# A feed-forward block in two stages through device memory, with seven-product multiplication on 512-token halves

## The reference

```python
h = _rmsnorm(x, P['norm_ffn_g'][layer]) * (1 + mod[:, 4]) + mod[:, 3]
gu = h @ P['ffn_w_gate_up'][layer]
x = x + mod[:, 5] * ((jax.nn.silu(gu[..., :FFN_HIDDEN]) * gu[..., FFN_HIDDEN:]) @ P['ffn_w_down'][layer])
```

## Time and profile before

| what | value |
|---|---|
| median of 3 runs | 2457.27 us (2455.51 to 2458.7) |
| the profiled execution's own time | 2461.06 us |
| its span, first to last instruction | 2459.3 us |
| PE busy | 2393.5 us (97%) |
| PEld (weight loads) busy | 2277.0 us (93%) |
| DVE, ACT, POOL busy | 1171.8, 693.8, 767.3 us |
| mean granted TensorE clock | 0.988 |

### The profile page before, as it was taken

The page is one execution under the profiler, slowest core; times in us unless marked ns, Lnnn a source line. Parts: engine busy times, 40 slices in busy tenths (PEclk is TensorE's granted clock), DMA queues, the critical chain, the costliest instruction groups (busy, mean ns, idle before and its releaser), DMA issues.

```text
span 2459.3 us, 37048 instructions
## 1 busy us (share of the span) xinstructions
PE 2393.5 (97%) x15703; PEld 2277.0 (93%) x15703; DVE 1171.8 (48%) x2225; ACT 693.8 (28%) x1056; POOL 767.3 (31%) x650
## 2 busy tenths in 40 slices
PE   7999998999999999999999999999999999999998
PEld 5997877678999999999999999988999999999998
DVE  5277653456444444344445411546544444444445
ACT  5122233426322222122224311144412222122224
POOL 3221120113244333334333332122443333433431
PEclk8999999999999999999999999999999999999999
DMA  9424342861221222222222678311111111111111
GB/s 305 161 67 144 118 138 77 295 236 35 69 86 57 79 71 86 69 86 86 69 86 69 213 269 296 119 36 35 35 52 46 41 52 52 35 52 52 52 52 71
DMA packets 163969, 249.12 MB, mean 101 GB/s; under 512 B 6164, under 2 KB 150825, under 8 KB 162526
## 3 DMA queue, kind: packets, MB, share of 16 engines
q1 hardware_dynamic: 150762, 179.29, 22.2%
q0 software_dynamic: 4784, 63.31, 7.4%
q10 hardware_dynamic: 8260, 4.15, 0.6%
HBM read 228.04 MB, written 62.54 MB: 118 GB/s over the span
## 4 chain that ended last, share of the span: by engine, by line
PE 76%; DVE 2%; ACT 1%; issue 0%; ACTq 0%; DVEq 0%
PE ps L2832 32%; PE ps L2872 12%; PE ps L2870 11%; PE ps L2871 11%; PE ps L3023 3%; PE ps L2976 3%; PE ps L3158 1%; DVE x L1870 1%; PE ps L3046 0%; PE ps L3350 0%; PE ps L3193 0%; PE ps L3367 0%; DVE nt L1909 0%; DVE tmp L2430 0%; PE ps L3313 0%
## 5 line engine op out<-in xcount | busy, mean ns | idle before, releaser
L2832 PE MATMUL ps<-h_hi,w_slot 128*128 128x352 f32 x2112 | 539.3, 329 | 6.1 <-ACT tmp L1389 2.9
L2630 POOL TENSOR_TENSOR w_slot<-w_raw,w_slot 128x512 fp32r<-128x512 f32 x240 | 303.9, 1298 | 682.0 <-DVE w_sum L2023 555.5
L2832 PE MATMUL ps<-f_hi,w_slot 128*128 128x352 f32 x1920 | 470.3, 324 | 0.0
L2872 PE MATMUL ps<-h_hi,w_slot 128*128 128x352 f32 x1280 | 413.3, 323 | 0.0
L2870 PE MATMUL ps<-h_hi,w_slot 128*128 128x352 f32 x1280 | 412.9, 323 | 0.0
L2871 PE MATMUL ps<-h_lo,w_slot 128*128 128x352 f32 x1280 | 411.2, 321 | 0.0
L1960 DVE SCALAR_TENSOR_TENSOR x<-ps,mod,x 128x704 f32<-128x704 f32 (+1 forms) x384 | 270.5, 746 | 290.8 <-PE ps L2832 290.2
L2832 PEld LDWEIGHTS ps<-h_hi,w_slot 128*128 128x128 f32 x2112 | 371.8, 189 | 25.3 <-issue 21.9
L2616 POOL TENSOR_TENSOR w_slot<-w_raw,w_slot 128x512 fp32r<-128x512 f32 x132 | 177.6, 1372 | 535.7 <-ACT w_slot L1384 527.2
L2832 PE MATMUL ps<-h_lo,w_slot 128*128 128x352 f32 x1056 | 340.2, 322 | 0.0
L2832 PEld LDWEIGHTS ps<-f_hi,w_slot 128*128 128x128 f32 x1920 | 334.2, 188 | 4.9 <-issue 4.1
(11 more groups left out here) (398 smaller groups left out, 3215.0 us busy)
## 6 DMA issues: line engine op xcount, KB each, us to landing
w_raw<-in_ada_w SPq DMA_DIRECT2D x48, 1024.0 KB, 6.0
w_raw<-in_ffn_w_gate_up SPq DMA_DIRECT2D x44, 1024.0 KB, 5.1
out_kv_sample<-in_cache_b_kv POOLq DMA_DIRECT2D x8, 4088.0 KB, 20.7
w_raw<-in_ffn_w_down SPq DMA_DIRECT2D x22, 1024.0 KB, 4.9
w_raw<-in_e_w_in SPq DMA_DIRECT2D x11, 1024.0 KB, 5.5
w_raw<-in_o_w_in SPq DMA_DIRECT2D x10, 1024.0 KB, 16.2
cache<-in_cache_b_kv SPq DMA_DIRECT2D x16, 512.0 KB, 6.1
out_kv_sample<-in_cache_b_kv POOLq DMA_DIRECT2D x8, 1016.0 KB, 8.8
```

The costliest lines, as they stand in the source:

```text
L2630: pool.tensor_tensor(w_slot[slot_of(it.raw)][:, c], w_raw[it.raw.slot][:, c], w_slot[it.hi[0]].bitcast(F32)[:, c], ALU.subtract).then_inc( ...
L2832: mm = pe.matmul(big(t)[:, b, 0:BLK], wt, xt[:, k, b * BLK:b * BLK + BLK], start=(k == 0 and n == 0), stop=(k == K - 1 and n == 2))
L2872: return pe.matmul(bank(it, j), w_low, x_high, start=False, stop=last, skip_group_check=True)
```

## The change

The feed-forward block goes in two stages.

Stage one makes gate and up of groups 1 to 10 as 20 units, one after the other, without down units between them. Each has seven products on the two halves of 512 prompt tokens, 84 matmuls of 512 columns; there is no direct block. The order of the products is 1, 2, 6, 4, 7, 5, 3, and products 6 and 7 accumulate in the PSUM bank of product 1, which ScalarE copies out after each of the three (`sum_copied`). Each unit uses three banks; the next uses the other three. Hidden values are stored to a scratch tensor in device memory, group by group, by SP (`store_f`), from the tile in which the next gate unit will write.

Stage two has 10 down units per layer for the hidden groups 0 to 9: five chunks of 512 hidden rows, each with two halves of 512 output channels. A chunk (2 MB) is loaded back by SP into the space of h_lo (`load_chunk`). VectorE makes four token sums of it (two operations of `chunk_sums` in each of two items), ScalarE five high parts (`chunk_high`), and GpSimd and VectorE the low parts. A down unit is 14 products of 6 matmuls of 512 columns, 84 in all, two output pairs (q) side by side in six banks. VectorE adds each product straight into x (`added`): 8 additions of 512 columns and 4 of 1,024 per unit. The down rows of group 10 stay a plain unit.

Samples leave the dense matmuls. For each seven-product unit they are the 32-column weights of full-float matmuls over 256 columns of the raw weight tile, packed in four column groups as the modulation units are: 8 matmuls and 2 transposes for a gate or up unit, twice 4 matmuls and 2 transposes for a down unit. ScalarE copies the rows, and VectorE reduces four partial sums. They read the raw weights, so they stand after product 6 of the unit before.

The modulation units of layer 0 stand after products 4 and 7 of units 1 to 10, two to a unit, and their weights go into the space of x, which is stored to memory at the start of the block and loaded back in unit 14.

The diff, cut to its core (`it` is a unit, `after` the next one, `before` the one before, `lefts` the count of VectorE's writes up to a unit):

```diff
+GATE_ORDER = (1, 2, 6, 4, 7, 5, 3)
+DOWN_ORDER = (1, 2, 6, 4, 5, 7, 3)
...
+        units = [seven(role, layer, g) for g in range(1, GROUPS) for role in ("f_gate", "f_up")]
+        units += [down_seven(layer, c, h) for c in range(CHUNKS) for h in range(2)]
...
+            for which in DOWN_ORDER if down else GATE_ORDER:
+                if which == 3 and after:
+                    sums_split(after)
+                items.append(Item("product", of=it, which=which))
...
+                elif which == 6 and after:
+                    sample_of(after)
+                elif which == 4:
...
+                    if after:
+                        split(after)
...
+                release(slot_of(it.raw), product_last(it, 4))
+                release(it.hi[0], product_last(it, 4))
...
+                release(it.sums[0], product_last(it, 3))
+                release(it.sums_hi[0], product_last(it, 3))
...
+            def store_f(layer, g, m):
+
+                sp.dma_start(d_f[:, 2 * g + m, :], tmp[:, m, :]).then_inc(f_stored, 16)
+
+            def load_chunk(it):
...
+                sp.dma_start(xr[:, 0:4, c], rows[:, :, FIRST]).then_inc(chunk_loaded[it.j % 2], 16)
+                sp.dma_start(xr[:, 4:8, c], rows[:, :, SECOND]).then_inc(chunk_loaded[it.j % 2], 16)
...
+                if which == 2:
+                    if it.role == "f_gate":
+                        dve.wait_ge(f_stored, 32 * (10 * it.layer + it.j))
+                    else:
+                        dve.wait_ge(gate_made, 10 * it.layer + it.j)
+                    dve.wait_ge(copied, 3 * it.n + 1)
+                    summed(it, 1, part_a, tmp_c11)
...
+                def added(q, m, c, src):
+
+                    m += 4 * it.g + 2 * q
+                    dst = x[:, m, c]
...
+                    dve.scalar_tensor_tensor(dst, src, mod[:, 6 * layer + it.gate, m, 0:1], dst, ALU.mult, ALU.add)\
+                        .then_inc(banks_left, 1)
...
+                    if which == 1:
+                        if first:
+                            pe.wait_ge(*all_left(before))
+                        else:
+                            pe.wait_ge(banks_left, before.lefts + 9 + q)
+                        pe.wait_ge(*left_low(2))
+                        pe.wait_ge(part_made, 4 * it.r + 2)
+                        straight(it, 0, q, 0, 0, rows(0))
...
+                    elif which == 6:
+                        pe.wait_ge(t_made, made + 5)
+                        pe.wait_ge(banks_left, it.lefts + 1 + q)
+                        of_sums(it, 0, q, 1, sums(T2), adds=True)
...
+                for k in range(count):
+                    j = S_TOK * (k % 4)
+                    mm = pe.matmul(misc(it.misc)[j:j + S_TOK, 0:256], rows[:, k, :], w[:, k, c],
+                                   start=(k < 4), stop=(k >= count - 4), skip_group_check=True)
+                mm.then_inc(misc_ready, 1)
```

More of the change, by code:

```diff
@@ L201, in make_plan @@
 def make_plan():
-    n = {"unit": 0, "big": 0, "misc": 0, "norm": 0, "seven": 0, "part": 0}
+    n = {"unit": 0, "big": 0, "misc": 0, "norm": 0, "seven": 0, "part": 0, "gu": 0, "fd": 0, "done": 0, "left": 0}
     def take(what, count=1):
@@ L521, in seven, with down_seven @@
         col = g if role == "f_gate" else GROUPS + g
-        return Item("seven", weights="ffn_w_gate_up", col=col, role=role, layer=layer, j=g, n=take("seven"))
+        return Item("seven", weights="ffn_w_gate_up", col=col, role=role, layer=layer, j=g, n=take("gu"), w=take("seven"),
+                    done=take("done", 7), lefts=take("left", 6))
+    def down_seven(layer, c, h):
+        return Item("seven", weights="ffn_w_down", role="f_down", layer=layer, j=c, g=h, gate=5, n=take("fd"), w=take("seven"),
+                    done=take("done", 14), lefts=take("left", 12))
     def split(it):
@@ L527, in split @@
         items.append(Item("split", of=it))
-        for half in range(2 if it.kind == "seven" else 0):
+        for half in range(2):
             items.append(Item("w_sums", of=it, which=half))
@@ new lines, in ffn, with adds, chunk @@
+        sums_split(units[0])
+        def adds(i, which):
+            if layer or not 1 <= i <= 10:
+                return
+            if which in (4, 7):
+                ada_units.append(Item("ada", k=len(ada_units), misc=take("misc")))
+                items.append(ada_units[-1])
+            else:
+                items.append(Item("ada_out", k=len(ada_units) - 1, misc=take("misc")))
+        def chunk(kind, c, which=0):
+            if c < CHUNKS:
+                items.append(Item(kind, layer=layer, j=c, which=which))
@@ L986, in build_trunk @@
         for i, it in enumerate(plan):
-            if it.kind == "down_tile":
+            if it.kind == "product":
                 break
@@ L1701, in _ @@
                     split_hi(ups[it.layer].unit + 1)
[L1702 to L1706 removed]
+                elif it.kind == "product" and it.of.role != "f_down":
+                    gate_product(it.of, it.which)
                 elif it.kind == "project":
@@ new lines, in product, with summed @@
+            def product(it, which, q=0):
+                dve.wait_ge(*product_done(it, which, q))
+            def summed(it, j, part, dst):
+                if it.role == "f_gate":
+                    dve.tensor_tensor(dst, bank(it, j), part, ALU.add).then_inc(banks_left, 1)
+                    return
+                to = bank(it, j) if dst is tmp_c21 else part
+                own(dve.tensor_tensor(to, bank(it, j), part, ALU.add))
+                dve.tensor_tensor(dst, to, dst, ALU.mult).then_inc(banks_left, 1)
@@ new lines, in three, with straight @@
+            def three(it, j, q, w_high, w_low, x_high, x_low, first, last):
+                pe.matmul(bank(it, j, q), w_high, x_high, start=first, stop=False, skip_group_check=True)
+                pe.matmul(bank(it, j, q), w_high, x_low, start=False, stop=False, skip_group_check=True)
+                return pe.matmul(bank(it, j, q), w_low, x_high, start=False, stop=last, skip_group_check=True)
+            def straight(it, j, q, k0, m, x, adds=False):
+                down = it.role == "f_down"
+                hi, lo = [w_slot[s].rearrange("p (k n) -> p k n", k=4 if down else KT) for s in (it.hi[0], slot_of(it.raw))]
+                count, m = 2 if down else 4, m + 2 * q
+                for k in range(count):
+                    x_high, x_low = x(k)
+                    c = slice(m * P, m * P + P)
+                    mm = three(it, j, q, hi[:, k0 + k, c], lo[:, k0 + k, c], x_high, x_low, k == 0 and not adds, k == count - 1)
+                mm.then_inc(products_done, 1)
@@ new lines, in of_sums @@
+            def of_sums(it, j, q, i, x, adds=False):
+                down = it.role == "f_down"
+                hi, lo = [w_slot[s].rearrange("p (s k n) -> p s k n", s=4, k=4) for s in (it.sums_hi[0], it.sums[0])]
+                pe.wait_ge(part_made, 4 * it.rs + (DOWN_SUMS if down else GATE_SUMS).index(i) + 1)
+                count = 2 if down else 4
+                for k in range(count):
+                    x_high, x_low = x(k)
+                    n = 2 * k + q if down else k
+                    mm = three(it, j, q, hi[:, i, n, :], lo[:, i, n, :], x_high, x_low, k == 0 and not adds, k == count - 1)
+                mm.then_inc(products_done, 1)
```

809 lines of the change are left out of this document (494 added, 315 removed).

## The result

The changed kernel takes **2542.0 us** (median of 4 runs, 2540.6 to 2549.0) against 2456.4 before (4 runs beside it): ratio 1.0358, 95% interval 1.0345 to 1.0371, so 3.6% slower. I had forecast 2414, faster, with 2458 as the upper end. The profiled execution has a span of 2540.2 us. SBUF is the on-chip memory in which the tiles stand, and PSUM holds TensorE's results, in banks.

A forecast was written before the change was run, and what follows sets the result against it. TensorE, busy 97% of the span, was taken as the bound. Per layer, dense gain 84.0 less samples 44.0 gave 80 in all; less stalls of 37, net 43: 2461.1 to about 2418, median 2414 us, range 2362 to 2458.

The forecast's parts named there:

- What a matmul costs: Dense matmuls of 512 columns: 0.227 us each, with a fixed surplus per matmul; dense gain 84.0 us per layer.
- Rival B: Weight load sets the pace now, so a 512-column matmul costs 0.2133 to 0.216; 2361 us, chance 0.18.
- Samples: Separate sample matmuls: 1.34 us per gate or up unit, 1.72 per down unit; cost 44.0 us per layer.
- Rival E: Four column groups of samples run one after another, 60 units x 2 us more; 2534 us, chance 0.01.
- (c): Down units: TensorE waits ahead of product 6 for VectorE's addition of product 1, 0.8 us at 8 places; 6.4 us.
- (d): Stall at the last additions before the final down unit: 0.9 x 2 = 1.8 us.
- (f): Gate units: the first sum waits until the hidden tile is stored, delaying product 4; 0.4 x 20 = 8 us.
- rival C: Gate units' wait for the stored hidden tile costs 3.2 us more each, 64 in all; 2478 us, chance 0.10.
- (a): Start of each block: product 6 waits behind ScalarE's high parts and copy of product 1; 3.3 x 2 = 6.6 us.
- (b): Passage from gate and up to down units: VectorE's queue of 14.1 us outlasts TensorE's 9.5; 4.6 x 2 = 9.2 us.
- (e): Layer 0's gate units 1 to 10: modulation weights land late in SP's queue; 5 us in all.
- Rival D: VectorE paces stage two: operations cost 10% more, each down unit waits 1.5 to 2 us; 2449 us, chance 0.11.

The follow-up runs named there:

- e1: Changed kernel with the seven products of layer 1's gate and up units cut to seven widths, 256 to 512 columns: 2473.5 us.
- e11: Changed kernel with stores on ScalarE's queue, first sums' high part earlier, token sums moved and GpSimd's row pieces split: 2484.0 us, ratio 1.0100.
- e7: Changed kernel with the first chunk's token sums made 4 us earlier, directly after the weight sums of the first down unit: 2553.0 us.
- e3: Changed kernel with 16 of GpSimd's 24 pieces per pair of down units cut to 16 columns: 2497.7 us, pair 45.5 us.
- e5: Changed kernel with ScalarE making the first weight sums' high part earlier at each block's start, ahead of T3's: 2533.0 us.
- e14: e13 with token sum T3 of the next chunk moved to the pair's second unit and GpSimd starting with rows 2 and 3: 2482.1 us.
- e9: Changed kernel with 16 of GpSimd's 24 subtractions per pair of down units replaced by full-size one-operand copies: 2512.0 us.
- e13: e11 with the chunk loads after the first issued from ScalarE's queue instead of SP's: 2488.6 us, ratio 1.0143.
- e4: Changed kernel with the stores of hidden rows issued by ScalarE instead of SP: 2529.8 us.

## Why the prediction was wrong

The miss is 2542 - 2414 = 128 us. By its steps, with what the trace shows for both layers together:

- **What a matmul costs.** The step that failed first. I took the fixed surplus, 0.227; it is 0.232, close to the proportional end, and e1 shows the proportion for seven widths. 5,040 x 0.005 = **25 us**. The reason I gave, that short full-float records come every 0.117 us, told of weight loads and nothing of whether the surplus goes by columns. Rival B, which lies on the other side, is refuted with it. So is, for this stream, the N / 2.4 + 2.5 ns of the Trainium skill's "TensorE: Matmul & The Clock Gate", section "Back-to-back issue gap".
- **Samples.** A gate or up unit 20.83 - 84 x 0.2325 (the distance within a product of that unit) = 1.30 against 1.34: right. A clean down unit (the last full one of e11, 21.45) 1.92 against 1.72: 4 us over 20 units. Rival E is out.
- **(c) Down units.** Predicted 6.4; measured 251.5 (from 2240.8 to 2492.3) - 10 x 21.45 = 37.0 per layer, 74 in all: **68 us**, half of the miss. The wait of (d) stands behind that stretch, 1.2 a layer against 0.9: **1 us**. I had the queue and its order right, even the place (product 6 waits for product 1's addition) and the number of times (8), but summed VectorE's instructions by durations taken in a gap where nothing ran beside them: 4.6 us for token sums that take 7.0, an end 0.8 us late that came 4.1 late. The step that failed is the unwritten one, that VectorE at 87% and GpSimd at 74% (24 pieces of 1.29 in two units) do not touch each other. By the sizes in this trace VectorE's instructions of a pair with two operands in SBUF are 7 x 1.22, 8 x 0.69 and 4 x 0.22, 14.9 us, and GpSimd's 24 pieces 30.2: together 45.1 of a clean pair's 42.9. This sum is an estimate, and somewhat high, since the two overlap a little where they meet: in e7 a sum and a piece by turns take 2.2 us and not 1.22 + 1.26. It says that there is hardly a place where a piece stands free; it is no floor that a run has shown. With GpSimd's pieces whole no pair in the middle of a block took less than 47.2; e3, at 45.5, had made two thirds of them nearly nothing. And a stall of 4 us brings half a clock with it, 2 us more, which I had in no term.
- **(f) Stores.** 8 predicted, 18 measured (0.6 to 0.9 in most gate units, up to 2.3, by their length beside an up unit's), **10 us**. That is rival C's mechanism, and its sign came in 18 of 20 gate units; but it would have needed 44 us more than my 8 to take the forecast gain.
- **(a) Starts** 6.6 predicted, 5.9 + 6.5 measured, the 4.7 us gap and the half clock behind it: **6 us**. e5 shows the chain was the one I named.
- **(b) Passage** 9.2 predicted, a gap of 8.8 instead of 0.2 per layer, 17.2, measured: **8 us**; T1 took 2.22 and a sample addition 0.98 there, beside GpSimd.
- **(e) Modulation weights** 5 predicted, no hole found. But the step "the modulation units move without a change in number, 0" was wrong: an up unit of layer 0 with its two takes 23.72, 2.89 more than one without, and in the earlier trace rows two of them cost 67.81 - 65.60 = 2.21. Standing singly costs 0.7 in each of 10 units, **7 us**, less the 5: 2.

These sum to 25 + 4 + 68 + 1 + 10 + 6 + 8 + 2 = 124 of 128. The other 4 I have not placed.

Rival D had the right engine, "VectorE paces stage two", and its sign came, a hole before product 6 in all 20 down units (4.1 us in eight of them). It had 2449 for it: it took 10% on each instruction where the trace shows 85% on those beside GpSimd. The range ended past D and left out C; nothing in it held several terms going wrong in one direction, and they did. For (c), the largest, the reason is shown: its durations came from rows of a stretch in which nothing or little ran beside them.

The gain side was also thinner than it looked. With 0.232 dense work per layer is 585, not 572, and with samples (26 + 19) 630 against 656: 26 us per layer, 52 in all, in exchange for every stall. The stalls that e11 did not remove (4.7 x 8 for pairs, 17 for passages) are 55 us by themselves. So the best versions found, e11 and e14, are still 1.0 and 1.2% slower than the kernel before by their runs; none of the 14 is faster, not even those that leave work out.

## What to carry to other kernels

Before adding work to VectorE or GpSimd, add up, per stage, VectorE's instructions with two operands in SBUF and GpSimd's that read SBUF (e9's copies with one operand count too), and hold the sum against the stage's length as if they were one engine; if it comes near, there is hardly a place where the two do not meet; a duration from a stretch where the other is silent is a lower bound. When such a stage stalls, move pieces so that the two engines' pieces part, and look at the other engine's row before moving anything into an idle stretch. A duration per matmul measured at one width says nothing of another until one width more has been seen.

## What I had not expected of the hardware

- VectorE's subtraction of 1,024 elements from two SBUF operands: 1.22 us alone, 2.2 to 2.3 beside GpSimd's subtractions; a sample addition of 64 elements 0.22 alone, up to 1.3. GpSimd's four pieces 5.03 alone, 7.76 when three of them meet such a subtraction (the changed kernel), 8.79 when all four do (e7). VectorE's additions with one PSUM operand: 0.74 with or without. Whoever comes second waits for the rest of the other's instruction, whichever engine it is (e9's copy 1.60 in place of 0.61 behind T4, and T3 1.62 in place of 1.22 behind that copy).
- Fast-float matmuls at the full clock cost 1.09 to 1.11 times N / 2.4 at every width from 256 to 512, while at the half clock show N / 1.2 with nothing on top (512 columns: 0.43 us). The Trainium skill, "TensorE: Matmul & The Clock Gate", section "Back-to-back issue gap", gives a fixed 2.5 ns for the gap of a matmul taken by itself; in this stream it is 19 ns at 512, and the measurement decides.
- Two queues did not make the chunk land sooner: 7.9 us in the median from ScalarE's queue (e13), 7.6 behind the weights in SP's (e11). The store, of half the size, did land sooner from ScalarE's queue, 5.2 us in place of 7.7 (e4).
